# Splitting GpSimd's subtractions for the low parts of U and V into four operations of a quarter of the columns

## The chip, the cores and the metric

One Trainium2 chip, one of its cores. The metric is the device time of one launch, in microseconds (us), median of the runs: 4199.21 us before (three runs, 4194.9 to 4211.27). Lower is better. The engines go by the profile's names: PE is TensorE's matrix multiply and PEld its weight load, DVE is VectorE, ACT is ScalarE, POOL is GpSimd, SP is SyncE, which here only issues transfers.

## The reference, cut to what matters

One inference step of a decoder layer: attention in two head groups for a prompt of 1024 tokens and for 32 decoding tokens, then a mixer that retrieves experts by product keys. The change lies in the last part, which is, for a block of tokens `tb`:

```python
e = i1 * N_KEYS + i2                       # 16 experts for each of 8 heads
g = softmax(cv)
a = gelu(einsum('td,thkd->thk', tb, u_tab[e]))
out = einsum('thk,thkd->td', g * a, v_tab[e])
```

There are 16384 experts, each with a row of 1024 in the table U and one in V. All is float32.

## The kernel before, in words

The kernel runs in stages (`project`, `prompt_attn`, `sample_attn`, `mix_out`, `peer_route`, `peer_experts`, `finish`), with a barrier between them. `peer_experts` works out the experts in two ways at once.

**The dense way, for 640 prompt tokens.** The gate of every expert for each of these tokens lies in memory (`s_g`). The 128 chunks of 128 experts are taken in 32 rounds of four chunks (`CQ`). TensorE computes at the precision of float32 from numbers split into a high and a low part: `split_product` (L1321 to L1323) is three multiplications, high by high, low by high, high by low. So each chunk of U (`uu`, 128 x 1024) and of V (`vv`) needs both parts. ScalarE copies it to the rounded high part (`split_u` L1933, `split_v` L1939), and GpSimd subtracts that from the chunk, which gives the low part (`low_u` L2074, `low_v` L2078). The 256 subtractions of the stage each cover 128 partitions and 1024 columns.

A round of TensorE has two phases of 192 matmuls each. Eight *dots* (m = 0 to 7, two for each chunk) multiply a chunk of U with half of the tokens. Sixteen *outs* (n = 0 to 15) multiply the four chunks of V with the weighed results. The dots of a chunk wait for its `ul`: m = 4 waits for the third chunk of the round and m = 6 for the fourth. The first out waits for the last `vl` of the round (L1907). Between them, ScalarE applies gelu (L1945) and VectorE multiplies with the gates (L2046). ScalarE copies the product to its high part (L1949), and VectorE subtracts that from it (L2049, both inputs in SBUF). VectorE also adds the result of each out to an accumulator (L2058, and L2060 in the first round). An out can start only when the one four before it has been added, as there are four PSUM buffers (`SUMS`).

**The gathered way, for the other 416 steps of 128 tokens and experts.** GpSimd gathers 128 rows of U and V by an indirect transfer (L2083) into one of four buffers (`RING`). It may do so when VectorE has finished the step four before. VectorE forms the dot of the row of U with the token's row (L2014, both inputs in SBUF). ScalarE makes a weight of it (L1964, L1966), and VectorE adds the weighed row of V to a PSUM tile (L2026, one input in SBUF, one in PSUM).

The order on each engine is written out by hand. GpSimd's order in a round is: V of chunk 0 (behind dot m = 0), gather, U of chunk 2 (m = 1), V of chunk 1 (m = 2), gather, U of chunk 3 (m = 3), gather, V of chunk 2 (m = 4), V of chunk 3 and gather (m = 5), gather (m = 7), and in the outs U of the next round's chunk 0 and gather (n = 0), U of chunk 1 and gather (n = 2), then six gathers. On VectorE a dot or a sum of the gathered way stands between the operations of the dense way (`share`), one or two to a slot. SP's queue loads the next chunks of U, of the gates and of V in this order, each when the buffer is free: for U that is `ul_done`, for V `vl_done` (L1883 to L1888).

Of the kernel before, what the change touches and what calls it, by code (L numbers as in the profile page):

```python
# [8 lines left out]
ALU = mybir.AluOpType  # L9
# [8 lines left out]
D = 1024  # L18
KC = D // P
# [104 lines left out]
def project(nc, io, keep):  # L124
# [15 lines left out]
    with ExitStack() as ctx:  # L140
# [103 lines left out]
        with nc.Block() as block:  # L244
# [151 lines left out]
            def _(pe):  # L396
# [41 lines left out]
                pe.wait_ge(silu_done, 1)  # L438
                NR = NMOD + 3 * KC + 1
                for k in range(KC):  # L440
                    nc.tensor.transpose(pT[:, k * NCOND:(k + 1) * NCOND], csilu[:, k * P:(k + 1) * P],
                                        keep.ident[0:NCOND, 0:NCOND])
                nc.tensor.transpose(pT[:, 128:128 + NR], names[0:NR, :], keep.ident[0:NR, 0:NR]).then_inc(turned, 1)
                pe.wait_ge(lam_one, 1)
# [1331 lines left out]
CQ = 4  # L1776
# [7 lines left out]
def peer_experts(nc, io, keep):  # L1784


    with ExitStack() as ctx:
        def sb(name, shape, dt=F32):
            return ctx.enter_context(nc.sbuf_tensor(name, shape, dt))

        uu = sb("e_u", [P, 2, KC, P])
        vv = sb("e_v", [P, 2, D])
        uh = sb("e_uh", [P, 2, KC, P], F32R)
        ul = sb("e_ul", [P, 2, KC, P], F32R)
# [5 lines left out]
        vh = sb("e_vh", [P, CQ, D], F32R)  # L1800

        vl = sb("e_vl", [P, CQ, D], F32R)
# [17 lines left out]
        ul_done = nc.alloc_semaphore("e_ul_done")  # L1820
        vh_done = nc.alloc_semaphore("e_vh_done")
        vl_done = nc.alloc_semaphore("e_vl_done")
# [15 lines left out]
        uview = io["peer_ut"]  # L1838
        vview = io["peer_uv"].rearrange("(c e) d -> c e d", e=NK)[:, :, D:2 * D]
        V_AT = (0, 2, 4, 5)  # L1840
        NR = 2 * STEPS // NQ
        assert NR * NQ == 2 * STEPS

        def share(slot):

            if slot >= DOTS:
                first = NR - OUTS + slot - DOTS
                return range(first, first + 1)
            return range((NR - OUTS) * slot // DOTS, (NR - OUTS) * (slot + 1) // DOTS)

        def dots_of(j):

            return None if j and j % 2 == 0 else (j + 1) // 2 if j + 1 < 2 * STEPS else None

        def sums_of(j):
            return (j // 2 - 1 if j and j % 2 == 0 else STEPS - 1 if j == 2 * STEPS - 1 else None)
# [13 lines left out]
        with nc.Block() as block:  # L1870
# [57 lines left out]
            def _(act):  # L1928
                def split_u(c):
                    act.wait_ge(u_in[c % 2], 16 * (c // 2) + 16)  # L1930
                    if c >= 2:
                        act.wait_ge(dotted, NBD * (c - 2) + NBD)
                    nc.scalar.activation(uh[:, c % 2], uu[:, c % 2], ACT.Copy).then_inc(uh_done, 1)  # L1933

                def split_v(c):
                    act.wait_ge(v_in[c % 2], 16 * (c // 2) + 16)
                    if c >= CQ:
                        act.wait_ge(summed, OUTS * (c // CQ))
                    nc.scalar.activation(vh[:, c % CQ], vv[:, c % 2], ACT.Copy).then_inc(vh_done, 1)  # L1939
# [28 lines left out]
                def gathers(i, slot):  # L1968
                    for j in share(slot):
                        s = dots_of(NR * i + j)  # L1970
                        if s is not None:
                            weigh(s)
                            if last_of(s) and s < STEPS - 1:
                                h_copy(tile_of(s) + 1)
                        s = sums_of(NR * i + j)
                        if s is not None and last_of(s):
                            t = tile_of(s)
                            act.wait_ge(row_added, s + 1)
                            if t:
                                act.wait_ge(grow_out, 16 * t)  # L1980
                            nc.scalar.activation(grow, pY[:], ACT.Copy).then_inc(grow_done, 1)
                            act.wait_ge(grow_done, t + 1)
                            act.dma_start(io["s_go"][t], grow).then_inc(grow_out, 16)
# [7 lines left out]
                for i in range(NQ):  # L1991
                    for m in range(DOTS):
                        gelus(i, m)
                        if m % NBD == 1 and m // NBD < 2:
                            split_u(CQ * i + 2 + m // NBD)
                        if m in V_AT:
                            split_v(CQ * i + V_AT.index(m))
                        gathers(i, m)
# [71 lines left out]
            @block.gpsimd  # L2070
            def _(pool):
                def low_u(c):
                    pool.wait_ge(uh_done, c + 1)
                    nc.gpsimd.tensor_tensor(ul[:, c % 2], uu[:, c % 2], uh[:, c % 2], ALU.subtract).then_inc(ul_done, 1)  # L2074

                def low_v(c):
                    pool.wait_ge(vh_done, c + 1)
                    nc.gpsimd.tensor_tensor(vl[:, c % CQ], vv[:, c % 2], vh[:, c % CQ], ALU.subtract).then_inc(vl_done, 1)  # L2078

                def gather(s):  # L2080
                    if s >= RING:
                        pool.wait_ge(row_added, s - RING + 1)
                    nc.gpsimd.indirect_dma_start(uv[:, s % RING], None, io["peer_uv"],  # L2083
                                                 bass.IndirectOffsetOnAxis(ap=keep.g_idx[:, s:s + 1], axis=0),
                                                 ).then_inc(uv_in[s % RING], 16)

                def gathers(i, slot):
                    for j in share(slot):
                        s = sums_of(NR * i + j)
                        if s is not None and s + RING < STEPS:  # L2090
                            gather(s + RING)

                low_u(0)
                low_u(1)
                for n in range(2):
                    pool.wait_ge(keep.g_stored[n], 16 * ND)
                pool.wait_ge(keep.spread_out, 2 * 16 * (P // TS))
                for s in range(RING):
                    gather(s)
                for i in range(NQ):  # L2100
                    for m in range(DOTS):
                        if m % NBD == 1 and m // NBD < 2:
                            low_u(CQ * i + 2 + m // NBD)
                        if m in V_AT:
                            low_v(CQ * i + V_AT.index(m))
                        gathers(i, m)
                    for n in range(OUTS):
                        if n in (0, 2) and i + 1 < NQ:
                            low_u(CQ * (i + 1) + n // 2)
                        gathers(i, DOTS + n)  # L2110
# [157 lines left out]
def build(nc, io):  # L2268
    keep = Keep()
    with ExitStack() as ctx:  # L2270
# [32 lines left out]
        for stage in (peer_experts, finish):  # L2303
            run_stage(nc, io, keep, stage)
# [41 lines left out]
```

## Time and profile before

| | before |
|---|---|
| median of three runs | 4199.21 us |
| the profiled execution | 4200.97 us, of which its span is 4199.4 us |
| PE busy | 3399.6 us, 81% of the span |
| DVE busy | 2807.4 us, 67% |
| POOL busy | 1690.8 us, 40% |
| ACT busy | 1338.2 us, 32% |
| mean granted clock of TensorE | 0.894 |

The times come from one profiled execution. A row of a timeline has the start in us from the beginning of the span, the duration in us, the engine, the line, the operation, what it writes and reads, and in brackets the idle time before it with what ended it. An operation that waits for something other than a semaphore, once it has been started, shows as a longer duration. A row of groups has the count, the busy time, the mean duration in ns, and the idle time of the engine ahead of the group.

### The profile page before, as it was taken

Reading aid. Unit: us, or ns where it says so; the run is one execution under the profiler, and the core shown is the slowest. Engines: PE = TensorE matmul, PEld = TensorE weight load, DVE = VectorE, ACT = ScalarE, POOL = GpSimd, SP = SyncE. Lnnn points to the kernel's source line nnn. Section 1 sums busy time; section 2 is a strip of 40 time slices with the busy share of each in tenths; the row PEclk is TensorE's granted clock in tenths of the full one; section 3 lists DMA queues with packets and bytes.
Section 4 is the critical chain, followed back from the end, with each engine's and each line's share of the span. In section 5 each row is a group of like instructions: output and inputs, shape, how many; then the busy total and the mean of one; then the engine's idle time right before and its main releaser. Section 6 shows DMA issues by size and latency. Waiting matters only on the chain. (4 is left out here: it accounts for less than half of the span.)

```text
span 4199.4 us, 59061 instructions
## 1 busy us (share of the span) xinstructions
PE 3399.6 (81%) x20585; PEld 2924.5 (70%) x20585; DVE 2807.4 (67%) x5853; ACT 1338.2 (32%) x3148; POOL 1690.8 (40%) x1333
## 2 busy tenths in 40 slices
PE   6799688466777688266659999999999999999995
PEld 3578455111544578255559999999999999998994
DVE  3114576001133129999969999889889989998885
ACT  3010466000011111386843333233333333333331
POOL 1011000000000443287865665565556555655650
PEclk8899799767679799676779999999999999999997
DMA  6765543999311233154578988888898889888883
GB/s 238 252 236 206 171 157 127 365 395 407 154 36 56 95 98 106 37 131 98 116 209 314 327 319 314 311 322 316 307 325 319 324 319 328 319 315 298 323 302 150
DMA packets 393741, 1001.85 MB, mean 239 GB/s; under 512 B 186980, under 2 KB 238031, under 8 KB 329752
## 3 DMA queue, kind: packets, MB, share of 16 engines
q1 hardware_dynamic: 327960, 491.18, 34.4%
q0 software_dynamic: 62656, 469.86, 30.9%
q10 hardware_dynamic: 2944, 38.77, 2.5%
q8 instruction: 68, 1.11, 0.1%
q14 instruction: 113, 0.93, 0.1%
HBM read 914.75 MB, written 152.04 MB: 254 GB/s over the span
## 5 line engine op out<-in xcount | busy, mean ns | idle before, releaser
L2014 DVE CUSTOM_DVE_ANT_0 e_uv<-e_uv,e_h 128x1024 f32<-128x1024 f32 x416 | 725.4, 1744 | 78.0 <-DMA e_uv<-peer_uv,k_g_idx 77.3
L2083 POOL DMA_INDIRECT e_uv<-peer_uv,k_g_idx x416 | 522.2, 1255 | 548.5 <-DVE e_pY L2026 507.3
L1321 PE MATMUL e_po<-e_ph,e_vh 128*128 128x320 f32 x2048 | 648.0, 316 | 64.5 <-DVE k_OT L2058 58.4
L1321 PE MATMUL e_pa<-k_hi_d,e_uh 128*128 128x320 f32 x2048 | 639.8, 312 | 50.3 <-POOL e_ul L2074 37.6
L1322 PE MATMUL e_pa<-k_lo_d,e_uh 128*128 128x320 f32 x2048 | 634.4, 310 | 0.0
L1323 PE MATMUL e_pa<-k_hi_d,e_ul 128*128 128x320 f32 x2048 | 634.3, 310 | 0.0
L1322 PE MATMUL e_po<-e_pl,e_vh 128*128 128x320 f32 x2048 | 633.4, 309 | 0.0
L1323 PE MATMUL e_po<-e_ph,e_vl 128*128 128x320 f32 x2048 | 633.4, 309 | 0.0
L2026 DVE SCALAR_TENSOR_TENSOR e_pY<-e_uv,e_wts,e_pY 128x1024 f32<-128x1024 f32 x412 | 525.7, 1276 | 0.0
L1321 PEld LDWEIGHTS e_po<-e_ph,e_vh 128*128 128x128 f32 x2048 | 384.9, 188 | 92.3 <-DVE k_OT L2058 75.9
L1321 PEld LDWEIGHTS e_pa<-k_hi_d,e_uh 128*128 128x128 f32 x2048 | 386.1, 189 | 62.1 <-issue 46.2
L1964 ACT ACTIVATE e_gel<-e_dots 128x1 f32<-128x1 f32 x416 | 83.9, 202 | 977.1 <-DVE e_dots L2014 977.1
L1322 PEld LDWEIGHTS e_pa<-k_lo_d,e_uh 128*128 128x128 f32 x2048 | 386.2, 189 | 0.0
L1323 PEld LDWEIGHTS e_pa<-k_hi_d,e_ul 128*128 128x128 f32 x2048 | 386.0, 188 | 0.0
L1322 PEld LDWEIGHTS e_po<-e_pl,e_vh 128*128 128x128 f32 x2048 | 385.3, 188 | 0.0
L1323 PEld LDWEIGHTS e_po<-e_ph,e_vl 128*128 128x128 f32 x2048 | 385.1, 188 | 0.0
L2074 POOL TENSOR_TENSOR e_ul<-e_u,e_uh 128x1024 fp32r<-128x1024 f32 x128 | 309.2, 2416 | 146.7 <-ACT e_uh L1933 146.1
L2078 POOL TENSOR_TENSOR e_vl<-e_v,e_vh 128x1024 fp32r<-128x1024 f32 x128 | 309.5, 2419 | 124.5 <-ACT e_vh L1939 123.5
L1772 PE MATMUL r_pG<-k_OT 128*128 128x128 f32 x1280 | 246.1, 359 | 138.7 <-DVE k_OT L1471 117.4
L1772 PEld LDWEIGHTS r_pG<-k_OT 128*128 128x128 f32 x1280 | 217.2, 258 | 168.1 <-DVE k_OT L1471 158.2
L1714 POOL TENSOR_SCALAR k_OT<-k_iota,r_second 128x128 f32<-128x128 f32 x480 | 329.8, 706 | 3.9 <-POOL r_second L1707 0.2
L2058 DVE TENSOR_TENSOR k_OT<-e_po,k_OT 128x320 f32<-128x320 f32 x496 | 237.9, 480 | 0.0
(284 smaller groups left out, 5863.9 us busy)
## 6 DMA issues: line engine op xcount, KB each, us to landing
s_kv<-kv_pages SPq DMA_DIRECT2D x128, 512.0 KB, 6.9
s_kv<-kv_state SPq DMA_DIRECT2D x32, 2048.0 KB, 17.3
e_v<-peer_uv SPq DMA_DIRECT2D x128, 512.0 KB, 6.3
e_u<-peer_ut SPq DMA_DIRECT2D x126, 512.0 KB, 6.2
s_g<-r_G SPq DMA_DIRECT2D x10, 4096.0 KB, 21.0
k_OT<-s_g SPq DMA_DIRECT2D x128, 320.0 KB, 5.5
k_win_sample<-state_k_win ACTq DMA_DIRECT2D x28, 1168.0 KB
v_win_sample<-state_v_win POOLq DMA_DIRECT2D x28, 1168.0 KB, 9.5
```

The source lines that it names most:

```text
L1321: nc.tensor.matmul(out, lhs_hi, rhs_hi, start=start, stop=False)
L1322: nc.tensor.matmul(out, lhs_hi, rhs_lo, start=False, stop=False)
L1323: return nc.tensor.matmul(out, lhs_lo, rhs_hi, start=False, stop=stop)
L1714: x = nc.gpsimd.tensor_scalar(hot2[:, u, t], keep.iota[:], second[:, u, t:t + 1], None, ALU.is_equal)
L1772: x = nc.tensor.matmul(pG[:, u, t], hot2[:, u, t], hot1[:, u, t], start=True, stop=True)
L1964: nc.scalar.activation(gel[:, r], dots[:, r], ACT.Gelu).then_inc(row_gelu, 1)
L2014: nc.vector.tensor_tensor_reduce(uv[:, r, 0:D], uv[:, r, 0:D], h[:], 1.0, 0.0, ALU.mult, ALU.add, dots[:, r:r + 1]).then_inc(row_dotted, 1)
L2026: x = nc.vector.scalar_tensor_tensor(out=pY[:], in0=uv[:, r, D:2 * D], scalar=wts[:, r:r + 1], in1=pY[:], op0=ALU.mult, op1=ALU.add)
L2058: x = nc.vector.tensor_tensor(acc[:, k, cols], po[:, n % SUMS, 0:WD], acc[:, k, cols], ALU.add)
L2074: nc.gpsimd.tensor_tensor(ul[:, c % 2], uu[:, c % 2], uh[:, c % 2], ALU.subtract).then_inc(ul_done, 1)
L2078: nc.gpsimd.tensor_tensor(vl[:, c % CQ], vv[:, c % 2], vh[:, c % CQ], ALU.subtract).then_inc(vl_done, 1)
L2083: nc.gpsimd.indirect_dma_start(uv[:, s % RING], None, io["peer_uv"], bass.IndirectOffsetOnAxis(ap=keep.g_idx[:, s:s + 1], axis=0),).then_i ...
```

## The change

Each subtraction becomes a loop of four: `low_u` takes two of the eight column blocks of 128 at a time, `low_v` 256 of the 1024 columns at a time. The wait stands ahead of the first of the four and the semaphore is raised by the last. Operands, values, buffers and the order on all engines stay as they are. The 256 operations of 1024 columns become 1024 operations of 256 columns.

```diff
@@ -1838,6 +1838,7 @@
         V_AT = (0, 2, 4, 5)
+        PIECES = 4
@@ -2071,11 +2072,17 @@
                 def low_u(c):
                     pool.wait_ge(uh_done, c + 1)
-                    nc.gpsimd.tensor_tensor(ul[:, c % 2], uu[:, c % 2], uh[:, c % 2], ALU.subtract).then_inc(ul_done, 1)
+                    for n in range(PIECES):
+                        k = slice(n * KC // PIECES, (n + 1) * KC // PIECES)
+                        x = nc.gpsimd.tensor_tensor(ul[:, c % 2, k], uu[:, c % 2, k], uh[:, c % 2, k], ALU.subtract)
+                    x.then_inc(ul_done, 1)

                 def low_v(c):
                     pool.wait_ge(vh_done, c + 1)
-                    nc.gpsimd.tensor_tensor(vl[:, c % CQ], vv[:, c % 2], vh[:, c % CQ], ALU.subtract).then_inc(vl_done, 1)
+                    for n in range(PIECES):
+                        d = slice(n * D // PIECES, (n + 1) * D // PIECES)
+                        x = nc.gpsimd.tensor_tensor(vl[:, c % CQ, d], vv[:, c % 2, d], vh[:, c % CQ, d], ALU.subtract)
+                    x.then_inc(vl_done, 1)
```

## Rows read from the trace of the kernel before

**Rows 1.** The windows view of the expert stage, from TensorE's first matmul to its last.
```profile
core 0: us, PE busy (x) PEld busy (x) DVE busy (x) ACT busy (x) POOL busy (x), PEclk, DMA share, GB/s
2169.40:4111.70 1942.30, 1847.89 (x12288) 1808.37 (x12288) 1735.15 (x2270) 661.25 (x1606) 1136.85 (x671) 1.00 0.89 317
3025.75:3054.60 28.85, 28.43 (x194) 28.13 (x193) 26.10 (x33) 13.86 (x30) 20.94 (x12) 1.00 0.88 320
3054.60:3085.30 30.70, 28.88 (x194) 28.21 (x193) 27.32 (x41) 6.67 (x20) 14.71 (x10) 1.00 0.91 327
```
**Rows 2.** Timeline of PE: end of the dots of round 14, and its two longest waits.
```profile
3054.16 0.31 PE L1321 MATMUL e_pa<-k_hi_d,e_uh 128*128 128x320 f32 x1
3054.60 0.34 PE L1321 MATMUL e_po<-e_ph,e_vh 128*128 128x320 f32 x1
...
3040.41 0.41 PE L1321 MATMUL e_pa<-k_hi_d,e_uh 128*128 128x320 f32 x1 [0.42 <-POOL e_ul L2074]
3070.34 0.41 PE L1321 MATMUL e_po<-e_ph,e_vh 128*128 128x320 f32 x1 [1.29 <-DVE k_OT L2058]
```
**Rows 3.** Groups of VectorE's and GpSimd's operations, and their shortest, median and longest duration.
```profile
L2014 DVE CUSTOM_DVE_ANT_0 e_uv<-e_uv,e_h 128x1024 f32<-128x1024 f32 x416 | 725.4, 1744 | 78.0 <-DMA e_uv<-peer_uv,k_g_idx 77.3
L2014 DVE CUSTOM_DVE_ANT_0 e_uv<-e_uv,e_h x416: 1205/1225/3182, 2183.8 to 4109.0; 128x1024 f32<-128x1024 f32 x139
L2049 DVE TENSOR_TENSOR e_pl<-e_act,e_ph x256: 478/482/3411, 2185.5 to 4086.7; 128x320 fp32r<-128x320 f32 x128
L2078 POOL TENSOR_TENSOR e_vl<-e_v,e_vh 128x1024 fp32r<-128x1024 f32 x128 | 309.5, 2419 | 124.5 <-ACT e_vh L1939 123.5
```
**Rows 4.** Timeline of POOL in round 14.
```profile
3033.51 2.43 POOL L2078 TENSOR_TENSOR e_vl<-e_v,e_vh 128x1024 fp32r<-128x1024 f32 x1 [3.35 <-ACT e_vh L1939]
3036.08 1.77 POOL L2083 DMA_INDIRECT e_uv<-peer_uv,k_g_idx  x1
3037.86 2.42 POOL L2074 TENSOR_TENSOR e_ul<-e_u,e_uh 128x1024 fp32r<-128x1024 f32 x1
3040.22 2.41 POOL L2078 TENSOR_TENSOR e_vl<-e_v,e_vh 128x1024 fp32r<-128x1024 f32 x1
3044.93 2.41 POOL L2074 TENSOR_TENSOR e_ul<-e_u,e_uh 128x1024 fp32r<-128x1024 f32 x1 [1.11 <-ACT e_uh L1933]
3051.98 2.42 POOL L2078 TENSOR_TENSOR e_vl<-e_v,e_vh 128x1024 fp32r<-128x1024 f32 x1 [0.29 <-ACT e_vh L1939]
3058.44 0.94 POOL L2083 DMA_INDIRECT e_uv<-peer_uv,k_g_idx  x1 [2.13 <-DVE e_pY L2026]
```
**Rows 5.** Timeline of DVE in round 14.
```profile
3034.27 2.75 DVE L2014 CUSTOM_DVE_ANT_0 e_uv<-e_uv,e_h 128x1024 f32<-128x1024 f32 x1
3039.62 3.37 DVE L2049 TENSOR_TENSOR e_pl<-e_act,e_ph 128x320 fp32r<-128x320 f32 x1
3059.63 0.48 DVE L2058 TENSOR_TENSOR k_OT<-e_po,k_OT 128x320 f32<-128x320 f32 x1
3062.45 2.33 DVE L2014 CUSTOM_DVE_ANT_0 e_uv<-e_uv,e_h 128x1024 f32<-128x1024 f32 x1 [0.76 <-DMA e_uv<-peer_uv,k_g_idx]
```
**Rows 6.** Timelines of POOL and DVE in two earlier stages: adjacent GpSimd operations.
```profile
364.09 4.63 POOL L584 TENSOR_TENSOR p_wlo<-p_raw,p_whi 128x2048 fp32r<-128x2048 f32 x1 [43.83 <-ACT p_whi L344]
368.68 5.06 POOL L584 TENSOR_TENSOR p_wlo<-p_raw,p_whi 128x2048 fp32r<-128x2048 f32 x1
364.43 4.84 DVE L532 TENSOR_TENSOR k_OT<-k_OT 128x512 f32<-128x512 f32 x1
...
1353.35 1.53 POOL L1314 TENSOR_TENSOR k_lo_d<-o_sq,k_hi_d 128x640 fp32r<-128x640 f32 x1 [276.88 <-ACT k_hi_g L1199]
1354.84 1.05 POOL L1315 TENSOR_TENSOR k_lo_g<-o_sq,k_hi_g 128x416 fp32r<-128x416 f32 x1
1353.38 1.54 DVE L1305 TENSOR_TENSOR o_sq<-o_sq,o_rstd 128x32 f32<-128x32 f32 x1
```
**Rows 7.** One GpSimd group of narrow operations: shortest, median and longest duration in ns.
```profile
L1714 POOL TENSOR_SCALAR k_OT<-k_iota,r_second x480: 595/602/2777, 1754.6 to 2143.9; 128x128 f32<-128x128 f32 x160
```

**Rows 8.** The waits view: us in total, times, longest.
```profile
PE e_po L1321 <- DVE k_OT L2058: 58.4, 60, 1.9
PE e_pa L1321 <- POOL e_ul L2074: 37.6, 33, 20.5
```

## The prediction

> **What bounds the kernel now.** I read the windows view first, for the stretch that the change touches. In the expert stage [rows 1] the clock is granted in full (1.00), TensorE is busy for 1847.89 of 1942.3 us and VectorE for 1735.15. GpSimd, whose work is changed, is busy for 1136.85. TensorE is the bound, but not free of waits. Matmuls that flow start 0.147 us apart ((3054.60 - 3054.16) / 3 [rows 2]), so the stage's 12288 need 12288 x 0.147 = 1806 us and some 136 us are waits, 4.3 us in each of the 32 rounds. In the round that I take as the example, the dots last 28.85 us and the outs 30.70 us, against 192 x 0.147 = 28.2 us for each [rows 1]: 0.6 us of waits in the dots and 2.5 in the outs.
>
> The timeline of TensorE names them [rows 2]: dot m = 4 waits for a low part of U from GpSimd, and an out waits for VectorE's addition of the out four before it. So GpSimd ends a wait in the dots, and VectorE in the outs.
>
> Why is VectorE late? The group of its row dots [rows 3] has a mean of 1744 ns against a median of 1225. The excess, (1744 - 1225) x 416 = 216 us, is time in which an operation had begun and got nowhere. The timelines show on what: a dot begins at 3034.27 while GpSimd subtracts (3033.51 + 2.43 = 3035.94), and ends at 3037.02, about 1.1 us after GpSimd [rows 4, 5]. That is its own length of 1.2, less a tenth. The operation L2049, which also reads two tensors from SBUF, takes 478 ns when free and up to 3411 [rows 3]. VectorE's operations with two inputs in SBUF stand still until GpSimd's subtraction is through.
>
> **What the change does, part by part.** It removes no work; it cuts each of these 2.4 us blocks into four. There are three terms.
>
> *The price of three more operations.* No row shows a two-input subtraction of 256 columns. The two nearest rows are of 640 columns (1.53 us) and of 416 (1.05), and the second starts at 1354.84, 0.04 before the first ends (1353.35 + 1.53) [rows 6]. The slope is 0.48 / 224 = 2.14 ns a column, so 256 columns take 1.05 - 160 x 0.00214 = 0.71 us, and four in a row 4 x 0.71 - 3 x 0.04 = 2.72 against 2.42: +0.3 us for each of the 256 operations. The lower end is nothing (a quarter of 2.42 each). The upper end comes from GpSimd's narrow operations, 602 ns for 128 columns with a single tensor as input [rows 7]: with 128 more columns 0.602 + 0.27 = 0.87 us, four in a row 3.4, +1.0. I take +0.3, since the two subtractions are the same kind of operation.
>
> *Does VectorE get in between two pieces?* The rows point both ways. In two earlier stages it does. A VectorE operation that began at 364.43 ended at 369.27, 0.59 us after the second of two adjacent subtractions had started (368.68), and that one took 5.06 us rather than 4.63: VectorE went first, and GpSimd paid 0.43. Likewise at 1354.84, between two operations with no wait between them, which is the form of the change: L1305, of only 32 columns, ended at 1354.92 [rows 6]. There are three such boundaries of the first kind and seven of the second. In the expert stage itself it does not. L2049 begins at 3039.62, while the third chunk's subtraction runs; the next starts at 3040.22 and ends at 3042.63, and L2049 ends at 3042.99, after both [rows 4, 5]. There are 31 such boundaries from 2202.85 to 4068.90, all the same. What differs is what went before. In the earlier stages GpSimd had been idle before the first of the pair. At 3037.86 it came straight from a gather. I take it that its parts are then out of step and never all free at once.
>
> The Trainium skill has a rule for this, in "GPSIMD Engine Reference", Instruction dispatch: GpSimd is eight cores, and each starts the next instruction when its own share of the last is finished, with nothing that holds them together. Taken alone it speaks against the change, since a boundary between pieces would be no gap for VectorE; that result is the first rival below. The trace agrees in the 31 boundaries and not in the other ten.
>
> Of the eight subtractions of a round, five begin after idle time ([rows 4] show three of them, at 3033.51, 3044.93 and 3051.98). So I expect VectorE to slip in for most of them, waiting at most one piece (0.7 us) where it now waits up to 2.4.
>
> *Who pays.* When VectorE slips in, GpSimd's remaining pieces wait for it. Today VectorE's held-up dot runs after the subtraction, beside the gather, which then takes 1.77 us instead of 0.94 [rows 4]. Only 0.8 of the 1.2 us falls on GpSimd. After the change the dot lies inside the subtraction and delays its end. The chain in the dots, from 3033.51 to 3051.98 + 2.42 = 3054.40, has TensorE close behind it at both ends. The third chunk of U is ready at 3040.28 and awaited (0.42 us of idle time [rows 2]), and the last V is ready at 3054.40, 0.2 us ahead of the first out at 3054.60.
>
> Step by step: V of chunk 0 ends at 3033.51 + 2.72 + 1.2 (the dot) = 3037.4. The gather, no longer blocked, ends 1.0 later at 3038.4. U of chunk 2 then takes 2.72, and 0.48 more for L2049 inside it: 3041.6 against 3040.28. Dot m = 4 loses 1.3. V of chunk 1, a gather and U of chunk 3 with a dot inside it: 3041.6 + 2.7 + 1.0 + 2.7 + 1.2 = 3049.2 against a moved need at 3047.5 + 1.3 = 3048.8: 0.4 lost. A gather, V of chunks 2 and 3 with one L2049 and one dot inside: 3049.2 + 1.0 + 2 x 2.7 + 0.5 + 1.2 = 3057.3. The first out would start at 3054.6 + 1.7 = 3056.3: 1.0 lost. Together the dots lose 2.7 us a round.
>
> What the outs get back is the relief of VectorE. Its first addition comes at 3059.63 although the out's last matmul started by 3054.60 + 12 x 0.147 = 3056.4 [rows 2, 5]; with TensorE 2.7 us later in the dots and VectorE's waits shorter, that lag is gone. The two dots that stand behind U's subtractions in the outs (as at 3062.45, 2.33 us long [rows 5]) lose about 1.0 us each now and some 0.4 then. Of the 2.5 us of waits in the outs I take 1.7 as gone. The rest stays, where an out waits for the last result of its own round and where a dot waits for a gather's rows (77.3 us in the stage [rows 3]).
>
> *The sum.* 2.7 - 1.7 = +1.0 us a round, 32 us in 32 rounds, and about 1 us for the first two subtractions, on which the stage's first matmul waits [rows 8]. The profiled execution took 4200.97 us (its span 4199.4 and 1.6 around it), 1.8 us above the median of the runs: 4201 + 33 = 4234 us.
>
> **The rivals.**
>
> *VectorE is held through all four pieces.* For it: the 31 boundaries, in this very stage. Against it: the ten others, one kind of which has exactly the change's form. Then every block lasts 2.72 instead of 2.42. U of chunk 2 comes after two longer operations (+0.6), the last V after four more, partly covered by idle times of 1.11 and 0.29 [rows 4] (+1.2 in the end for the first out). In the outs VectorE loses 2 x 0.3. That is +1.8 to +2.4 a round: 4201 + 2.4 x 32 = 4278 us.
>
> *VectorE's relief wins.* Its operations come earlier, and so do ScalarE's copies behind them and GpSimd's own starts: U of chunk 3 starts at 3044.93 only because L2049 was held until 3042.99. If pieces and intrusions lengthen the dots by only 0.5 a round, and the outs lose 2.2 of their 2.5 us of waits, the result is -1.7 x 32 = -54: 4147 us. For it: VectorE's 216 us of standing still in the dots alone, the largest waste in the stage. Against it: TensorE waits for GpSimd with no slack at m = 4 and the first out.
>
> *Both sides cancel.* The dots lose what the outs gain: 4201 us. Nothing in the profile speaks against it, as both terms are near 2 us a round.
>
> *Slower for another reason: a dear piece.* If a piece costs the upper end, +1.0 for each subtraction, the chain from V of chunk 0 to V of chunk 3 grows by 6 x 1.0 less 1.4 of idle time, 4.6 us a round before any intrusion, less the 1.7 given back: 2.9 x 32 = +93, 4294 us. It decides as soon as four pieces take more than 3.2 us.
>
> **How the numbers follow.** 0.5% (21 us) is about what a measurement of this kernel can tell from no change; that is 0.66 us a round. Forecast 0.38 (its own range 4205 to 4275, a fifth of it under the bound), held through 0.18, relief wins 0.24, cancel 0.15, dear piece 0.05. Slower: 0.38 x 0.8 + 0.18 + 0.05 = 0.53; same: 0.15 + 0.38 x 0.2 = 0.23; faster 0.24. The range reaches from within the relief case (4150) to beyond the held case (4290).
>
> **What would show it.** *The piece:* L2074 and L2078 with 512 operations each, of about 0.7 us where VectorE doesn't intrude. *Slipping in:* L2014's longest duration falls from 3182 ns to about 1.9 us, its mean to about 1.45, and some pieces take over 1.5 us. If it is held through, the mean rises above 1744. *Who pays:* TensorE's idle time for L2074, 37.6 us of which the first wait of the stage is 20.5, rises by over 40 us, a wait for L2078 at the first out appears beside it, and that for L2058 falls from 58.4 us to under 30 [rows 8]. *Wrong* would be a subtraction of four pieces that ends within 2.8 us of its start although VectorE got in, or waits in the dots that don't grow: then the time falls below 4180.

## The result and the profile after

The changed kernel takes 4312.22 us (median of four runs, 4310.29 to 4320.06), the kernel before 4197.06 (four runs). The ratio is 1.0272, 95% interval 1.0244 to 1.03: 115 us slower, where 33 us slower were forecast, and above the range.

| | before | after |
|---|---|---|
| the profiled execution, its span | 4200.97, 4199.4 us | 4320.06, 4318.5 us |
| the expert stage, first to last matmul | 1942.3 us | 2052.8 us |
| VectorE busy in it | 1735.15 us | 1548.07 us |
| GpSimd busy in it | 1136.85 us | 1309.64 us |
| granted clock in it | 1.00 | 0.96 |

The windows view of the stage, and the groups of its operations (page of the changed kernel), answer to [rows 1, 3, 8]:

```profile
2179.60:4232.40 2052.80, 1896.63 (x12288) 1863.84 (x12288) 1548.07 (x2270) 671.18 (x1605) 1309.64 (x1436) 0.96 0.84 300
```
```profile
L1321 PE MATMUL e_pa<-k_hi_d,e_uh 128*128 128x320 f32 x2048 | 667.3, 326 | 149.9 <-POOL e_ul L2077 132.9
L1322 PE MATMUL e_pa<-k_lo_d,e_uh 128*128 128x320 f32 x2048 | 659.2, 322 | 0.0
L1321 PE MATMUL e_po<-e_ph,e_vh 128*128 128x320 f32 x2048 | 640.7, 313 | 27.0 <-DVE k_OT L2059 20.4
L2015 DVE CUSTOM_DVE_ANT_0 e_uv<-e_uv,e_h 128x1024 f32<-128x1024 f32 x416 | 560.0, 1346 | 161.2 <-DMA e_uv<-peer_uv,k_g_idx 160.5
L2090 POOL DMA_INDIRECT e_uv<-peer_uv,k_g_idx x416 | 414.3, 996 | 526.9 <-DVE e_pY L2027 474.9
L2077 POOL TENSOR_TENSOR e_ul<-e_u,e_uh 128x256 fp32r<-128x256 f32 x512 | 467.4, 943 | 93.3 <-ACT e_uh L1934 91.2
L2084 POOL TENSOR_TENSOR e_vl<-e_v,e_vh 128x256 fp32r<-128x256 f32 x512 | 431.9, 875 | 136.6 <-ACT e_vh L1940 136.0
```

The stage is 110.5 us longer, and the profiled executions differ by 119 us: the stage also starts 10 us later (2179.6 instead of 2169.4). In the stage VectorE did get its relief: a row dot takes 1346 ns instead of 1744, and TensorE's waits for its additions fall from 58.4 to 20.4 us. Two things came in exchange. TensorE's waits for the low part of U rose from 37.6 to 132.9 us, and VectorE's waits for gathered rows from 77.3 to 160.5.

One round shows the rest. These are timelines of GpSimd, VectorE, TensorE and ScalarE in round 13 of the changed kernel; `x4` is four pieces in a row, and `...` stands for rows left out:

```profile
3021.91 4.08 POOL L2084 TENSOR_TENSOR e_vl<-e_v,e_vh 128x256 fp32r<-128x256 f32 x4 [3.34 <-ACT e_vh L1940]
3026.13 0.95 POOL L2090 DMA_INDIRECT e_uv<-peer_uv,k_g_idx  x1
3027.10 4.39 POOL L2077 TENSOR_TENSOR e_ul<-e_u,e_uh 128x256 fp32r<-128x256 f32 x4
...
3035.39 2.79 POOL L2077 TENSOR_TENSOR e_ul<-e_u,e_uh 128x256 fp32r<-128x256 f32 x4
...
3040.76 2.85 POOL L2084 TENSOR_TENSOR e_vl<-e_v,e_vh 128x256 fp32r<-128x256 f32 x4 [1.48 <-ACT e_vh L1940]
3044.27 3.81 POOL L2084 TENSOR_TENSOR e_vl<-e_v,e_vh 128x256 fp32r<-128x256 f32 x4 [0.66 <-ACT e_vh L1940]
```
```profile
3022.66 1.77 DVE L2015 CUSTOM_DVE_ANT_0 e_uv<-e_uv,e_h 128x1024 f32<-128x1024 f32 x1
...
3028.78 1.22 DVE L2015 CUSTOM_DVE_ANT_0 e_uv<-e_uv,e_h 128x1024 f32<-128x1024 f32 x1
...
3029.92 1.00 DVE L2050 TENSOR_TENSOR e_pl<-e_act,e_ph 128x320 fp32r<-128x320 f32 x1
```
```profile
3031.62 0.63 PE L1321 MATMUL e_pa<-k_hi_d,e_uh 128*128 128x320 f32 x1 [3.82 <-POOL e_ul L2077]
...
3038.21 0.42 ACT L1946 ACTIVATE e_pa<-e_pa 128x320 f32<-128x320 f32 x1 [3.69 <-PE e_pa L1323]
3039.63 1.05 ACT L1940 ACTIVATE e_vh<-e_v 128x1024 fp32r<-128x1024 f32 x1
```

Four pieces alone take 2.79 us. V of chunk 0 takes 4.08, since the dot of 3022.66 is inside it. U of chunk 2 takes 4.39: the dot of 3028.78 got in with no wait at all (1.22 us is its free length), and L2050 after it. So dot m = 4 waits 3.82 us. What comes next was in no step of the forecast. ScalarE's gelu of dot m = 4 starts at 3038.21, and only behind it comes the copy of V of chunk 2 (3039.63), on which GpSimd waits 1.48 us. And dot m = 4 itself is slow, as the windows view (TensorE's clock is the number after the POOL column) shows for the dots before the wait, the wait, dot m = 4 and the dots after it:

```profile
3020.61:3027.70 7.09, 7.09 (x50) 6.93 (x48) 6.63 (x9) 5.21 (x10) 5.62 (x6) 1.00 0.49 165
3027.70:3031.60 3.90, 0.11 (x1) 0.00 (x0) 3.23 (x5) 0.89 (x2) 3.90 (x5) 0.92 0.92 331
3031.62:3038.00 6.38, 6.38 (x24) 6.38 (x25) 0.50 (x1) 1.44 (x3) 6.20 (x9) 0.52 0.76 263
3038.00:3045.00 7.00, 7.00 (x50) 7.00 (x49) 4.12 (x7) 4.07 (x8) 4.71 (x8) 1.00 0.94 365
```

The granted clock of dot m = 4 is 0.52, near the lower of the two levels, 1.2 GHz, after TensorE had stood idle for 3.8 us; its 24 matmuls take 6.4 us instead of 3.5. This round is worse than the mean one; on average dot m = 5 starts 5.5 us behind m = 4, as the table shows.

The means over rounds 1 to 31, in us from the first matmul of the round, worked out from the starts and ends in each timeline, are the measure for all that follows ("ready" is the end of the last piece, and the other columns are starts; the last is the length of the round):

| kernel | U of chunk 2 ready | dot m = 4 | dot m = 5 | V of chunk 3 ready | first out | round |
|---|---|---|---|---|---|---|
| before | 15.0 | 15.2 | 18.8 | 29.4 | 29.6 | 60.6 |
| after | 18.2 | 18.3 | 23.8 | 34.1 | 34.6 | 64.1 |

The dots lost 5.0 us a round and the outs won 1.5 (31.0 to 29.5): 3.5 x 32 = 112 us.

### The profile page after: what moved, and what is told of

Same layout as the page of the kernel before. It is cut to its first block and busy times, and to the rows that moved or that the text cites. A ratio compares the mean times of both kernels' runs of the same rounds, so it can differ in the third digit from the quotient of the medians.

```text
span 4318.5 us, 59829 instructions
## 1 busy us (share of the span) xinstructions
PE 3438.2 (80%) x20585; PEld 2976.9 (69%) x20585; DVE 2627.0 (61%) x5853; ACT 1348.3 (31%) x3148; POOL 1864.1 (43%) x2101
## 3 DMA queue, kind: packets, MB, share of 16 engines
q1 hardware_dynamic: 327960, 491.18, 34.1%
q0 software_dynamic: 62656, 469.86, 29.5%
## 5 line engine op out<-in xcount | busy, mean ns | idle before, releaser
L1321 PE MATMUL e_pa<-k_hi_d,e_uh 128*128 128x320 f32 x2048 | 667.3, 326 | 149.9 <-POOL e_ul L2077 132.9
L1321 PE MATMUL e_po<-e_ph,e_vh 128*128 128x320 f32 x2048 | 640.7, 313 | 27.0 <-DVE k_OT L2059 20.4
L1322 PE MATMUL e_pa<-k_lo_d,e_uh 128*128 128x320 f32 x2048 | 659.2, 322 | 0.0
L1323 PE MATMUL e_pa<-k_hi_d,e_ul 128*128 128x320 f32 x2048 | 658.3, 321 | 0.0
L2015 DVE CUSTOM_DVE_ANT_0 e_uv<-e_uv,e_h 128x1024 f32<-128x1024 f32 x416 | 560.0, 1346 | 161.2 <-DMA e_uv<-peer_uv,k_g_idx 160.5
L2090 POOL DMA_INDIRECT e_uv<-peer_uv,k_g_idx x416 | 414.3, 996 | 526.9 <-DVE e_pY L2027 474.9
L1321 PEld LDWEIGHTS e_pa<-k_hi_d,e_uh 128*128 128x128 f32 x2048 | 409.4, 200 | 163.8 <-issue 136.0
L2077 POOL TENSOR_TENSOR e_ul<-e_u,e_uh 128x256 fp32r<-128x256 f32 x512 | 467.4, 943 | 93.3 <-ACT e_uh L1934 91.2
L2084 POOL TENSOR_TENSOR e_vl<-e_v,e_vh 128x256 fp32r<-128x256 f32 x512 | 431.9, 875 | 136.6 <-ACT e_vh L1940 136.0
L1322 PEld LDWEIGHTS e_pa<-k_lo_d,e_uh 128*128 128x128 f32 x2048 | 409.6, 200 | 0.0
L2047 DVE TENSOR_TENSOR e_act<-e_pa,k_OT 128x320 f32<-128x320 f32 x256 | 125.7, 491 | 365.6 <-ACT e_pa L1946 332.1
```

The source lines that it names most:

```text
L1321: nc.tensor.matmul(out, lhs_hi, rhs_hi, start=start, stop=False)
L1322: nc.tensor.matmul(out, lhs_hi, rhs_lo, start=False, stop=False)
L1323: return nc.tensor.matmul(out, lhs_lo, rhs_hi, start=False, stop=stop)
L2015: nc.vector.tensor_tensor_reduce(uv[:, r, 0:D], uv[:, r, 0:D], h[:], 1.0, 0.0, ALU.mult, ALU.add, dots[:, r:r + 1]).then_inc(row_dotted, 1)
L2047: nc.vector.tensor_tensor(act_out[:, m % 2], pa[:, m % 2, 0:WD], G[:, c % 2, cols], ALU.mult).then_inc(p_done, 1)
L2077: x = nc.gpsimd.tensor_tensor(ul[:, c % 2, k], uu[:, c % 2, k], uh[:, c % 2, k], ALU.subtract)
```

## Experiments

Each was timed against the kernel before on the same chip, whose median lay between 4184.5 and 4198.6; so I compare the ratios. The changed kernel's is 1.0272. One caution for small differences: in the profiled executions of all these kernels the expert stage starts between 2164.6 and 2183.4 us, though the edits touch nothing ahead of it but the first two subtractions, which they lengthen by at most 1 us. So a difference of 20 us between two of these executions need not come from the stage.

**Which part costs.** `e1_u_only` cuts the low parts of U only, `e2_v_only` those of V only:

```diff
+                    for n in range(1):        # in low_v (e1), in low_u (e2)
```

> Only the low parts of U are cut into four; those of V stay whole. Theory (the cost is a row dot that gets into V of chunk 0 and another into U of chunk 2, both ahead of dot m = 4, and the fall of TensorE's clock after that wait): V of chunk 0 lasts 2.4 us as before, the gather behind it is blocked (1.77 us) and U of chunk 2 follows straight from it, a start after which VectorE was held at 30 of 31 boundaries in the changed kernel. So U of chunk 2 lasts 2.8 and not 4.1 us, m = 4 waits about 1.0 us, hardly any matmul is slow, and the outs still gain their 1.5 us a round: about 4197 - 0.8 x 32 = 4170 us. Rival (the price of the extra operations, 0.38 us each, is the loss): half of the operations are cut, so half of the loss: 4255 us. Rival (intrusion into U alone is what counts): U of chunk 2 again lasts over 4 us and the time is near 4290.

> Only the low parts of V are cut into four. Theory: V of chunk 0 lasts 4.0 us with a dot inside, then an unblocked gather (0.95) and U of chunk 2 whole (2.4): ready about 1.7 us earlier than in the changed kernel, so m = 4 waits 3.7 - 1.7 = 2.0 us, and some of its matmuls are slow (0.5 us a round); the outs gain about half: (1.4 + 0.5 - 0.7) x 32 = +38: 4235 us. Rival (price): 4255 with V's half of the operations, and the wait at m = 4 grows by 0.4 us only.

Measured: 1.0114 (1.008 to 1.0149), 48 us slower; and 1.0183 (1.0145 to 1.0221), 77 us slower. They add up to 125, near the whole. My theory (4170 us) and the rival of the intrusion into U (4290) missed on e1, while the 4255 us of the price lie inside the interval (4231 to 4260). The places tell more than the time: dot m = 4 came only 0.4 us later, as my theory said, but a new wait of 1.4 us a round came at m = 6, since U of chunk 3 now has a dot inside it (3.84 us on average). So my account of m = 4 alone was too narrow. In e2, where theory (4235) and price (4255) are both below the interval, dot m = 4 starts 0.9 us later than before the change, m = 6 1.9 and the first out 2.1: two waits of about 1 us, at m = 4 and m = 6, and hardly one at the first out.

**The cut where nothing waits for the result.** `e3_outs_only` cuts only U of the next round's chunks 0 and 1:

```diff
+                    pieces = PIECES if c % CQ < 2 else 1    # low_u; low_v whole
```

> Only the two low parts of U that are computed in the outs (chunks 0 and 1 of the next round) are cut into four; the other six of a round stay whole. Theory: nothing waits for these two soon, so VectorE's relief costs nothing there: L2050's and the dots' waits in the dots phase and the wait at m = 4 stay as before (0.7 us a round), and the outs' waits fall from 3.0 us a round to about 1.5: 4197 - 1.5 x 32 = 4150 us. Rival (price): a quarter of the operations is cut and the result is between 4197 and 4225. Rival (the relief needs the dots phase): the outs' waits stay above 2.5 us a round, 4190 to 4200 us.

Measured: 1.0023 (1.0005 to 1.0041). The expected 47 us did not come. The waits view of e3 shows where they went:

```profile
DVE e_uv L2015 <- DMA e_uv<-peer_uv,k_g_idx: 150.0, 139, 3.4
PE e_po L1321 <- DVE k_OT L2059: 39.8, 64, 1.7
```

TensorE's waits for additions fall from 58.4 to 39.8 us, but VectorE, held less by GpSimd, now waits 150 instead of 77.3 us for gathered rows [rows 3]. The gather is issued behind the subtraction, which got longer (3.8 us instead of 2.4). So relief turned into that wait, which is the likely reason that nothing was won. Two smaller things show in the same profile: the cut was not free in the dots (the first out starts at 30.0 instead of 29.6), and the outs won 0.65 us a round, which left the stage 6.8 us shorter; the measured time shows nothing of that.

**The price without the intrusions.** `e5_uneven` keeps four operations but puts all boundaries at the start:

```diff
+        EDGES = (0, 16, 32, 48, D)
+                        k = slice(*EDGES[n:n + 2])     # columns of a piece, U flattened
```

> Four operations as in the change, but of 16, 16, 16 and 976 columns: the number of operations is the same, and the last three boundaries lie within the first 0.6 us of the block, so VectorE is hardly ever waiting at one and stands still for the rest, as before the change. It measures the price of the operations without the intrusions. Theory (the chain of GpSimd's work in the dots bounds the round, and both the pieces' price and the intrusions lengthen it): each block lasts 2.8 instead of 2.4 us and none lasts 4; the dots lose about 1.6 us a round and the outs gain nothing: 4197 + 1.6 x 32 = 4248 us. Rival (intrusions alone cost): within 10 us of 4197. Rival (price alone costs): the changed kernel's 4312.

Measured: 1.018 (1.0151 to 1.0208), 76 us slower: more than the theory's 4248 us, and far less than the 4312 of the price alone. The blocks take 2.8 us, most with nothing inside, and VectorE's dots are held longer than before the change, 1954 ns each (page of e5):

```profile
L2020 DVE CUSTOM_DVE_ANT_0 e_uv<-e_uv,e_h 128x1024 f32<-128x1024 f32 x416 | 812.9, 1954 | 106.4 <-DMA e_uv<-peer_uv,k_g_idx 105.3
L1321 PE MATMUL e_pa<-k_hi_d,e_uh 128*128 128x320 f32 x2048 | 644.4, 315 | 85.8 <-POOL e_ul L2082 77.1
```

So 0.4 us a block cost 76 us by the medians (51 by the rounds of the profiled execution, which are 62.2 us long, with the first out at 31.4); four even pieces, with relief and intrusions, cost 39 more by the medians. `e6_two` cuts into two halves:

```diff
+        PIECES = 2
```

> Two operations of half of the columns instead of four. One boundary in the middle of each block, a third of the price (0.13 us a block). Theory: a dot that arrives in the first half gets in at the middle, and no second VectorE operation does, so V of chunk 0 lasts 3.7 and U of chunk 2 about 3.7 us; the wait at m = 4 is about 2.7 us: the dots lose 3 and the outs gain 1.2 us a round: 4255 us. Rival (price): 4197 + 115 / 3 = 4235 us. Rival (more boundaries help): below 4197.

Measured: 1.0053 (1.003 to 1.0076), 21 us slower, nearest to the rival that counts the price (4235 us, still outside the interval). The dots lose 1.9 us a round and the outs win 1.9 (round 60.6 as before). The profiled execution is 15.6 us longer than before the change, but its expert stage only 2.9 (1945.2 against 1942.3); the stage starts at 2182.7 us instead of 2169.4. So by this profile two halves cost the stage nearly nothing, and what lies ahead of it makes up the difference; whether that holds for the other executions no profile shows. In e5 7.9 us lie ahead of the stage in the same way.

**Is it the wait at m = 4?** `e4_filler` fills that wait with unused matmuls:

```diff
+                        if c == 2:
+                            pe.wait_ge(added, OUTS * i + SUMS)
+                            for _ in range(22):
+                                nc.tensor.matmul(po[:, SUMS - 1, 0:WD], keep.hi_d[:, 0, 0:P], keep.hi_d[:, KC - 1, WD:DT], start=True, stop=True)
                         dot(i, c)
```

> The changed kernel, with 22 matmuls of 320 columns whose result is never used (stationary and moving operand the high part of the tokens, output the PSUM bank of the last out) ahead of dot m = 4 of every round, where TensorE waits 3.7 us. They fill 22 x 0.147 = 3.2 us of the wait. Theory (after the wait the clock falls to half and m = 4 lasts up to 6.4 us instead of 3.7, which costs 1.7 us a round): the wait that is left is short, no matmul of m = 4 is slow, and the time falls by 1.7 x 32 = 53 us, to about 4260, or to 4280 if in some rounds the fill is longer than the wait. Rival (the slow matmuls come from something else, as contention for SBUF with four short operations, or the load of the transfers): the slow matmuls stay, and the time stays at 4312 or above.

Measured: 1.0298 (1.0262 to 1.0334). Half of the theory held: the clock was 1.00 in the stage, the matmuls of the dots had 310 ns again instead of 322, and dot m = 5 started 3.6 us after m = 4 instead of 5.5. But the time did not fall. One reason is in the blocks: with the wait filled, U of chunk 3 takes 4.0 us instead of 3.0, since VectorE's operations now fall into it, and the six blocks from V of chunk 0 to V of chunk 3 sum to 22.4 us instead of 20.7. TensorE's groups in e4 show that it waits for V instead, 29.3 us against 3.2:

```profile
L1321 PE MATMUL e_po<-e_ph,e_vh 128*128 128x320 f32 x2048 | 641.4, 313 | 50.9 <-POOL e_vl L2089 29.3 <-DVE k_OT L2064 19.6 <-DVE k_OT L2066 1.1
L1322 PE MATMUL e_pa<-k_lo_d,e_uh 128*128 128x320 f32 x2047 | 633.8, 310 | 0.0
```

`e9_early_whole` leaves V of chunk 0 and U of chunk 2 whole, `e11_u2_whole` only U of chunk 2, and `e10_v2_earlier` moves V of chunk 2 ahead of dot m = 4's gelu:

```diff
+                    pieces = 1 if c % CQ == 2 else PIECES    # low_u in e9 and e11
+                    pieces = 1 if c % CQ == 0 else PIECES    # low_v in e9
+        V_AT = (0, 2, 3, 5)                                  # e10
```

> The changed kernel with V of chunk 0 and U of chunk 2, the two ahead of dot m = 4, left whole; the other six of a round are cut into four. Theory: nothing gets into those two, so the wait at m = 4 is 0.7 us as before and its matmuls are not slow; but V of chunks 1, 2 and 3 and U of chunk 3 are still lengthened, and the first out waits for V of chunk 3, or m = 6 for U of chunk 3, some 1.5 us a round, against 1.0 gained in the outs: about 4215 us. Rival (the wait at m = 4 is the whole loss): the outs' gain is left, 4150 us. Rival (price alone): 4197 + 0.75 x 115 = 4283 us.

> The changed kernel with U of chunk 2 alone left whole, the one that dot m = 4 waits for. Theory: the row dot and the L2049 operation that get into it, and its price, are gone: it lasts 2.4 instead of 4.1 us, and m = 4 waits 1.7 us less with no slow matmuls. But the two VectorE operations now come behind it and lengthen what follows, so that of the 3.4 us (1.7 of wait, 1.7 of slow matmuls) only about 1 us a round comes back: 4280 us. Rival (the term that was left out, the dot in U of chunk 2, explains all that the forecast missed): 4197 + 32 x 1.0 = 4235 us.

> The changed kernel with V of chunk 2 computed one slot earlier on ScalarE and GpSimd (slot m = 3 instead of m = 4). In the changed kernel ScalarE's copy for it stands behind the gelu of dot m = 4, which ends late, and GpSimd idles 1.5 us before V of chunk 2 and 0.7 before V of chunk 3. Theory (the dots are bound by a loop: GpSimd's chain delays dot m = 4, and that delays ScalarE's copy and so the rest of the chain): the idle times go, the chain ends up to 1.5 us a round earlier, and the time falls by 30 to 50 us to about 4270. Rival (TensorE's wait at m = 4 is simply added to the round, what follows has slack): the time stays within 15 us of 4312.

Measured: e9 1.0147 (1.0115 to 1.0178), its wait at m = 4 as small as before the change and the first out at 32.2, 2.6 us late: between the theory's 4215 us and the price's 4283. e11 1.0269 (1.0242 to 1.0295), e10 1.0371 (1.0351 to 1.0391). In e11, dot m = 4 came 2.1 us earlier (16.2) and the first out only 0.3 (34.3): V of chunk 1 took 4.33 us, and U of chunk 3 4.07, because VectorE operations were in them instead of in U of chunk 2. My expectation of 1 us for that was wrong, and the one for e10 too. There V of chunk 2 was computed at once behind U of chunk 3, V of chunk 3 was ready at 34.2 as before, and the outs lost 1.0 us.

**Two limits side by side.** After e4, e10 and e11 I took GpSimd's whole chain as the limit (theory A). `e14_after_no_v1` takes one block out of it, behind m = 4, and `e15_before_no_v1` does so in the kernel before:

```diff
+                    few = c % CQ == 1 and c > CQ
+                    for n in range(1 if few else PIECES):
+                        d = slice(0, 16) if few else slice(n * D // PIECES, (n + 1) * D // PIECES)
```

> The changed kernel, but from the second round on the low part of V of chunk 1 is computed for 16 of its 1024 columns only, in one operation (the rest keeps the values of the first round, so a part of the result's correction is left out). This subtraction stands behind U of chunk 2 on GpSimd, so it can't shorten the wait at dot m = 4; it takes some 2.9 us out of GpSimd's chain from V of chunk 0 to V of chunk 3. Theory A (the length of that whole chain sets when the first out starts, 25.3 us in the changed kernel, and the waits along it only show where TensorE meets it): the chain falls to 22.4 us, the dots by 2.5 us a round, the time by 80 us to about 4232. Theory B (the wait at m = 4 and the slow matmuls behind it are what is lost): the time stays within 15 us of 4312.

> The kernel before the change with the same part left out: the low part of V of chunk 1 for 16 columns only from the second round on. Theory A: in this kernel GpSimd's chain has 2.1 us of idle time and waits for ScalarE's copies at U of chunk 3 and V of chunk 3, so an operation less shortens it hardly; what is gained is VectorE's hold of 3.4 us over it: between 10 and 40 us less, 4170. The effect is at most half of that in the changed kernel. Theory B: the same effect in both kernels.

Measured: 1.0261 (1.0235 to 1.0287) and 0.9973 (0.996 to 0.9986). Theory A fell: with 2.5 us of work less on GpSimd the first out came at 34.3 instead of 34.6. TensorE itself is the reason: from dot m = 4 (18.2) to the first out it has only 0.2 us of waits in the changed kernel, so what GpSimd does behind U of chunk 2 can't by itself bring the first out forward. The clock of 0.96 and the wait at m = 4 were as in the changed kernel (windows of the stage and TensorE's group in e14):

```profile
2200.00:4100.00 1900.00, 1767.27 (x11496) 1741.16 (x11495) 1426.48 (x2128) 628.78 (x1503) 1146.19 (x1260) 0.96 0.84 304
```
```profile
L1321 PE MATMUL e_pa<-k_hi_d,e_uh 128*128 128x320 f32 x2048 | 667.5, 326 | 143.6 <-POOL e_ul L2077 128.1 <-DVE e_act L2047 15.4
```

So taking away either limit alone gave next to nothing back. `e16_no_v1_filler` joins e4 and e14, and `e17_no_v1_u2_whole` joins e11 and e14 (the same edits together):

> The changed kernel with both: the 22 unused matmuls ahead of dot m = 4 (with which no matmul is slow), and the low part of V of chunk 1 computed for 16 columns only from the second round on. Each alone left the time where it was. Theory C (two limits of nearly the same length hold the dots: the latency through dot m = 4, which ends late and slow and on whose gelu ScalarE's copy of V of chunk 2 waits, and the sum of GpSimd's work up to V of chunk 3; with one gone the other binds): with both gone the first out comes 1.2 us earlier at least, a ratio to the kernel before of 1.018 or less instead of 1.026 to 1.03. Rival D (neither has anything to do with it; the outs or the gathered rows set the round): 1.026 or more.

> The changed kernel with both: U of chunk 2 whole (alone: ratio 1.027) and the low part of V of chunk 1 for 16 columns only from the second round on (alone: 1.026). Theory C: U of chunk 2 is ready 2.2 us earlier, so the latency through m = 4 goes, and GpSimd's chain is 3 to 4 us shorter: the first out comes 2 to 2.5 us earlier, the ratio is 1.008 to 1.013. Rival D: 1.025 or more. A result at 1.02 would mean that each contributes a little and they add.

| | alone | with V of chunk 1 left out (alone 1.0261) |
|---|---|---|
| filler at m = 4 | 1.0298 | 1.0174 (1.0151 to 1.0197) |
| U of chunk 2 whole | 1.0269 | 1.0181 (1.0152 to 1.0209) |

Both pairs win about 1%, where the single edits won 0.1% at most. That is what theory C says and rival D excludes; e17 came out less good than I expected from C (1.008 to 1.013), with the first out at 33.1 instead of 32 (32.9 in e16). The stages of the profiled executions agree, less sharply: 2052.8 us in the changed kernel, 2047.0 in e4, 2043.8 in e11 and 2034.6 in e14 (on a chip on which the kernel before is 13 us faster), but 1991.7 in e16 and 2000.8 in e17.

**Does VectorE get over a boundary?** `e7_gather_later` moves the gather of slot m = 0 behind U of chunk 2, in the kernel before:

```diff
-                        gathers(i, m)
+                        if m:
+                            gathers(i, m)
+                        if m == 1:
+                            gathers(i, 0)
```

> The kernel before the change with whole subtractions, with one gather of each round (that of slot m = 0) issued behind U of chunk 2 instead of ahead of it. So V of chunk 0, U of chunk 2 and V of chunk 1 are adjacent and begin after idle time. Theory 1 (a gather that was blocked itself leaves GpSimd's parts out of step, and only then is VectorE held over a boundary): the dot that waits for V of chunk 0 gets in at the boundary to U of chunk 2, and L2049, which was held for 3.4 us over the boundary of U of chunk 2 and V of chunk 1 in 31 of 31 cases, isn't any more where the two are adjacent. U of chunk 2 is ready 0.6 us earlier, and the time falls by 1 to 1.5 us a round, to about 4160. Rival (it is the lead of 0.5 us, or the place in the round, that decides): L2049 is held as before, and the time stays within 15 us of 4197. Rival (the gather that is later is missed): VectorE waits longer for gathered rows and the time rises by 20 us or more.

Measured: 1.0061 (1.0039 to 1.0082), 26 us slower where the theory said 37 faster. The third rival has the number but not by its cause: VectorE's waits for gathered rows fell from 77.3 to 38.9 us. Half of the loss lies in the stage (12.2 us in the profile), where dot m = 6 comes 0.8 us later. The edit set the gather between U of chunk 2 and V of chunk 1, so the boundary that I named was not tested. The one of V of chunk 0 and U of chunk 2 was, and there VectorE got in 29 times and was passed over none (timeline of GpSimd, the 3.40 us hold a dot of 1.2):

```profile
3049.36 2.42 POOL L2078 TENSOR_TENSOR e_vl<-e_v,e_vh 128x1024 fp32r<-128x1024 f32 x1 [3.34 <-ACT e_vh L1939]
3051.74 3.40 POOL L2074 TENSOR_TENSOR e_ul<-e_u,e_uh 128x1024 fp32r<-128x1024 f32 x1
```

**Other ways to win.** `e12_late_u` moves U's two subtractions of the outs later, `e13_late_u_split` also cuts them:

```diff
+        U_AT = (6, 10)
+                        if n in U_AT and i + 1 < NQ:
```

> The kernel before the change, whole subtractions, with U of the next round's chunks 0 and 1 moved from the outs n = 0 and 2 to n = 6 and 10, on ScalarE and GpSimd. Theory (the wait of 1.5 us at out n = 8 comes of two blocked dots on top of the lag with which VectorE enters the outs; later in the outs VectorE has caught up and four PSUM buffers cover a blocked dot): the waits at n = 8 and 10 fall by 1 us a round or more: 4165 us. Rival (the blocked dot costs the same wherever it is): 4197. Rival (the next load of U starts later and is missed in the dots): above 4210.

> As the kernel with U moved to the outs n = 6 and 10, and these two subtractions cut into four, the other six whole. Theory (a cut is harmless where nothing waits for its result, but its relief comes back as waits for gathered rows): within 8 us of the kernel with the move alone. Rival (the relief is worth its 1.5 us a round once the lag is gone): 20 us or more below it.

Measured: 1.0108 (1.009 to 1.0127) and 1.013 (1.011 to 1.0151). The waits at n = 8 went as expected (1.2 us a round before, none now), but dot m = 2 waits 2.0 us a round instead of 0.3, there for VectorE's L2047. The rival above 4210 us has the number, but its cause, a load of U that is missed, doesn't show: TensorE's waits for U's low part are 42.9 us against 37.6. The cut on top was harmless and useless, as expected. No kernel of the study beats the one before with all its work done.

## Why the prediction was wrong

The direction, the places and the mechanism were right; the size was not, 1.0 us a round forecast and 3.5 measured. By its steps:

*The price* was +0.3 us a block; it is +0.4 (2.79 to 2.84 against 2.42). One piece alone takes 0.71 us, as the slope from the two nearest rows said; the four in a row are 0.1 longer than forecast.

*VectorE slips in*: right. The dot's mean fell to 1346 (forecast 1450). The longest did not fall to 1.9 us but stayed at 3.2, because in 11 cases, 4 dots and 7 of L2050, VectorE was held to the end of a block. Where GpSimd began after idle time, VectorE got in at every boundary at which it waited (110 of 110 in the changed kernel, counted over the timeline); where it came straight from a gather, at 87 (fewer or more by how short a wait one counts) and was passed over at 38.

*Who pays*: the failed step. I charged U of chunk 2 with one L2049 of 0.48 us, 3.2 in all; it takes 4.14 on average, since a dot of 1.2 gets in too. Dot m = 4 lost 3.1 us (15.2 to 18.3), not 1.3. Of the 1.8 us that were missing, U of chunk 2 is 1.0. Another 0.5 is a term that I had put at nothing: V of chunk 0 starts at 8.8 us instead of 8.2, because ScalarE reaches the gelu of dot m = 0 that much later (6.2 instead of 5.7), for a reason that no experiment looked for. The last 0.3 is V of chunk 0 itself (4.06 us, not 3.9) and the gather behind it. The later blocks were overcharged in turn: U of chunk 3 has 2.96, not 3.9. The six blocks sum to 20.6 us, and 20.9 were forecast. So the sum of GpSimd's work came out right, in part by luck, since errors of 1 us in both directions cancel in it, and its distribution was wrong: what came early hit the place without slack. From m = 4 to the first out 1.4 us were forecast and 1.9 measured, but not by the forecast's cause: they are the slow matmuls of dot m = 4 (m = 5 starts 5.5 instead of 3.6 us later), a term that the forecast did not have, and GpSimd's chain then has idle time on ScalarE's copy behind that dot. The wait for V at the first out, which the forecast named as a sign, did not come (3.2 us in the whole stage). What e4, e14, e16 and e17 show in place of the forecast's single chain: this latency and GpSimd's own chain are two limits of nearly the same length, 34 us from the start of the round.

*The outs*: 1.7 forecast, 1.5 measured. But e3, which cuts only what is computed there, got 0.65 of it and no time.

*The rivals.* "Held through" was priced at 77 us, and e5, in which VectorE is in fact mostly held through, cost 76. It was not what the change did, and the match is partly luck: the rival lost 1.8 us in the dots and 0.6 in the outs, where e5's profile has 1.8 and nothing (30.8 us against 31.0), so that its rounds give 51 us. Its place in the range shows what I did wrong: with every block 0.4 us longer the dots already lose 1.8 us (first out at 31.4), and intrusions must come on top, yet I priced the case with intrusions below it. The relief could not pay for both.

## What to carry to other kernels

Cutting an operation to free a shared port makes room for others inside it, and so delays its end: first ask who waits for the end, and look for slack there, not at the victim's total of standing still. When two chains of nearly the same length run side by side, an edit that shortens one shows nothing; take both away before calling either harmless. Price the case without the benefit first; a forecast with more inside the same chain can't be cheaper unless the benefit lies on that chain.

## What the runs showed of the hardware

TensorE's granted clock fell to 0.52 for dot m = 4 after 3.8 us of idle time. In the kernel before the outs wait some 1.3 us in nearly every round, and at most 2 of the matmuls behind such a wait were slow (counted in the timeline); the stage's clock was 1.00. But two longer waits of that kernel, of 2.37 and 1.88 us, were followed by 11 and 13 slow matmuls, and the windows view has the granted clock behind them (0.51 and 0.64):

```profile
3393.70:3397.20 3.50, 3.44 (x13) 3.44 (x14) 3.22 (x5) 2.83 (x5) 1.96 (x1) 0.51 0.59 241
3986.60:3990.40 3.80, 3.72 (x17) 3.72 (x18) 3.80 (x7) 0.69 (x3) 0.94 (x1) 0.64 0.84 315
```

In the changed kernel the slow matmuls of the dots (starts more than 0.17 and less than 0.4 us apart, what exceeds 0.147 us each) cost 62 us, against 8 before, and over the whole stage 72 against 26. Filling the wait took them away, but the time did not fall.

A VectorE operation with two SBUF inputs holds GpSimd for its whole length and the other way round. The Trainium skill, "SBUF — State Buffer", Who interferes with whom, says that such an operation contends with a GpSimd operation that reads SBUF, that the shared port is an exclusive lock, and that the issue order decides who is blocked. The traces agree (2.79 and 4.08 us for the same four pieces), and show that after idle time every boundary is a new contest (110 of 110).

What decides at the boundaries of a block that comes straight from a gather is open. Forecast and e7 held that GpSimd's parts are then out of step, and that a gather that was blocked itself (1.77 us) is needed for it. In the changed kernel 30 of the 38 boundaries passed over follow such a gather, but with two halves (e6) 138 boundaries were passed over behind gathers of 1.0 us, so the second part is not true in general. The Trainium skill, "GPSIMD Engine Reference", Instruction dispatch, would explain parts out of step; no run here shows them.
